# Fourteen gate tiles in seven pairs by seven products of quarters, in a fused two-block kernel

## The reference, cut to what matters

```python
proj = h @ w_in                      # 1024 -> 8456; the last 3072 columns are gm
ua = (ya * silu(ga)) @ w_up_a        # 512 -> 1024, likewise ub, uc
gates = sigmoid(gm.reshape(B, S, 3, D))
merged = gates[:, :, 0] * ua + gates[:, :, 1] * ub + gates[:, :, 2] * uc
x = x + merged @ w_o
# second block: mixers, x + y @ w_out, x + conv_ffn, then
x = x + sigmoid(x @ ple_w_gate) * (p @ ple_w_proj)
return rmsnorm(x) * final_norm_gain
```

## Time and profile before

| | us |
|---|---|
| median of 3 runs | 1244.85 (1244.41 to 1246.07) |
| time of the profiled execution | 1245.98 |
| its span, first to last instruction | 1244.2 |
| busy: PE, PEld, DVE, ACT, POOL | 1226.6, 980.8, 644.1, 553.3, 663.6 |

### The profile page before, as it was taken

The page is one execution under the profiler, slowest core; times in us unless marked ns, Lnnn a source line. Parts: engine busy times, 40 slices in busy tenths (PEclk is TensorE's granted clock), DMA queues, the critical chain, the costliest instruction groups (busy, mean ns, idle before and its releaser), DMA issues.

```text
span 1244.2 us, 17041 instructions
## 1 busy us (share of the span) xinstructions
PE 1226.6 (99%) x6262; PEld 980.8 (79%) x6262; DVE 644.1 (52%) x1101; ACT 553.3 (44%) x1078; POOL 663.6 (53%) x499
## 2 busy tenths in 40 slices
PE   9999999999999999999999999999999999999997
PEld 7977777777878888887787777878888888788886
DVE  5555326757624221144587655478999999100024
ACT  6355545676634333245634665533232323322344
POOL 6573222363256444445294556556776667655542
PEclk9999999999999999999999999999999999999999
DMA  7332222122233333353142123323333333433321
GB/s 247 92 91 71 62 66 61 51 71 75 60 85 94 101 93 95 87 166 112 41 116 62 42 75 93 102 68 102 96 90 95 94 102 89 119 95 98 96 81 68
DMA packets 62426, 112.14 MB, mean 90 GB/s; under 512 B 6856, under 2 KB 11464, under 8 KB 62344
## 3 DMA queue, kind: packets, MB, share of 16 engines
q1 hardware_dynamic: 62200, 111.06, 31.2%
q10 hardware_dynamic: 144, 0.00, 0.0%
HBM read 108.87 MB, written 2.16 MB: 89 GB/s over the span
## 4 chain that ended last, share of the span: by engine, by line
PE 91%; DVE 5%; ACT 3%; issue 1%; DMA 0%; POOL 0%; SPq 0%; DVEq 0%; ACTq 0%; POOLq 0%
PE pb L972 25%; PE pb L973 25%; PE pb L975 25%; PE pb L1131 2%; PE pb L1107 2%; PE pb L1074 1%; PE pb L1028 1%; PE pb L1026 1%; PE pb L1045 1%; PE pb L1047 1%; PE pb L1046 1%; PE pb L1096 1%; PE pb L996 1%; PE pb L992 1%; PE pb L994 1%
## 5 line engine op out<-in xcount | busy, mean ns | idle before, releaser
L2288 POOL TENSOR_TENSOR wlo<-raw,whi 128x512 fp32r<-128x512 f32 (+3 forms) x395 | 544.4, 1392 | 435.9 <-ACT whi L1313 435.6
L972 PE MATMUL pb<-HH,whi 128*128 128x512 f32 x968 | 389.7, 403 | 0.0
L973 PE MATMUL pb<-HL,whi 128*128 128x512 f32 x968 | 382.8, 395 | 0.0
L975 PE MATMUL pb<-HH,wlo 128*128 128x512 f32 x968 | 381.6, 394 | 0.0
L1313 ACT ACTIVATE whi<-raw 128x512 fp32r<-128x512 f32 (+3 forms) x395 | 234.7, 615 | 179.6 <-PE pb L975 138.6
L972 PEld LDWEIGHTS pb<-HH,whi 128*128 128x128 f32 x968 | 182.3, 188 | 47.2 <-issue 4.6
L973 PEld LDWEIGHTS pb<-HL,whi 128*128 128x128 f32 x968 | 182.1, 188 | 43.1 <-issue 2.9
L975 PEld LDWEIGHTS pb<-HH,wlo 128*128 128x128 f32 x968 | 182.0, 188 | 42.4
L1738 DVE SCALAR_TENSOR_TENSOR cv<-zf,vecs,cv 128x512 f32<-128x512 f32 x88 | 124.7, 1417 | 3.1
L1397 ACT ACTIVATE P<-P,stat 128x256 f32<-128x256 f32 (+3 forms) x96 | 50.6, 527 | 82.0 <-DVE stat L1862 59.6
L1729 DVE TENSOR_TENSOR X<-pb,X 128x512 f32<-128x512 f32 x24 | 16.6, 690 | 134.3 <-PE pb L975 133.9
(11 more groups left out here) (393 smaller groups left out, 1910.3 us busy)
## 6 DMA issues: line engine op xcount, KB each, us to landing
raw<-in_wall SPq DMA_DIRECT2D x368, 256.0 KB, 2.7
raw<-in_wall SPq DMA_DIRECT2D x8, 260.0 KB, 3.0
X<-in_xT SPq DMA_DIRECT2D x8, 256.0 KB, 5.4
X<-in_xT SPq DMA_DIRECT2D x2, 1024.0 KB, 7.6
outT<-PP SPq DMA_DIRECT2D x8, 256.0 KB, 2.5
raw<-in_wall SPq DMA_DIRECT2D x10, 192.0 KB, 2.4
raw<-in_wall SPq DMA_DIRECT2D x9, 128.0 KB, 2.2
cst<-in_cst SPq DMA_DIRECT2D x1, 832.0 KB, 7.4
```

The source lines that it names most:

```text
L972: pe.do.matmul(b, hi, xh[k], start=start, stop=False)
L973: pe.do.matmul(b, hi, xl[k], start=False, stop=False)
L975: m = pe.do.matmul(b, lo, xh[k], start=False, stop=stop)
L2288: g.do.tensor_tensor(lo, x, hi.bitcast(F32), ALU.subtract).then_inc(*up(name, point))
```

## The change

Fourteen of the fifteen gate tiles with d >= 3 are taken in seven pairs. For a pair the two weight tiles (1024 x 128 each) are cut along the inputs into halves: A11 and A12 of the one, A21 and A22 of the other; the activations into four quarters, inputs by tokens. Seven products of 512 inputs by 256 tokens give both tiles: the weight factors are A11, A22, S2, S1, S3, A12 and S4 (S1 = A21 + A22, S2 = S1 - A11, S3 = A11 - A21, S4 = A12 - S2). VectorE forms S1 to S4 in fp32 from the loaded quarters, ScalarE rounds them, GpSimd writes their low parts (VectorE that of S3). The sums of the activations are formed once, in four steps `t_sums`, by VectorE, ScalarE and GpSimd. The products go to banks 3 to 7; VectorE adds them in fp32 (`from_bank`), ScalarE takes the tanh. Blocks d = 4 and d = 6 hold two pairs in a row, d = 3, 5 and 7 one; gm(3, 0) stays a plain tile. The up tiles rotate through banks 0 to 2. SyncE refills a slot only after the sums that read it.

Other edits: kC runs its four high products, then the four with the low activations, then the four with low weights; the decay matmul has 64 rows, with zeros below the four; `sums` stands one step later; in the hgrn part the scaled copies (`query_copy`), the two halves of `inverse`, the levels, the first scores and the merges of scores move, and one of four near queries goes from VectorE to ScalarE; `square_a(2)` moves ahead of eight pauses; the gate of the last half tile is made by Exp, + 1, reciprocal and product on VectorE, and the tables are loaded once at the end, not three times.

```diff
+PAIRS = [((3, 1), (3, 2)), ((4, 0), (4, 1)), ((4, 2), (5, 0)), ((5, 1), (5, 2)), ((6, 0), (6, 1)), ((6, 2), (7, 0)),
+         ((7, 1), (7, 2))]
+PAIRS_OF = {3: (0,), 4: (1, 2), 5: (3,), 6: (4, 5), 7: (6,)}
+FACTORS = ("A11", "A22", "S2", "S1", "S3", "A12", "S4")
...
-        if d >= 3:
-            for j in range(3):
-                fm("win", GM + 1024 * j + P * d)
+        if d == 3:
+            fm("win", gm_col(3, 0))
+        for p in PAIRS_OF.get(d, ()):
+            for col, k0 in quarters(p).values():
+                fm4(col, k0)
...
+    def pair(self, p):
+        for i, x in enumerate("abcde"):
+            self.hold(3 + i, ("acc", p, x))
+        for x in FACTORS:
+            self.split_to(self.unit_of[p, x] + LOOK)
+            self.add("product7", p, x)
...
-            if i == 1:
+            if i == 2:
...
-            if d >= 3:
-                for j in range(3):
-                    gm(d, j)
+            if d == 3:
+                gm(3, 0)
+            for p in PAIRS_OF.get(d, ()):
+                self.pair(p)
...
-                take("main", ("up", n, d))
+                take("ups", ("up", n, d))
...
+            if d < 2:
+                add("t_sums", 2 + d)
...
+        copies = {(1, 4): ("query_copy", 0), (2, 1): ("inverse", 0), (2, 4): ("query_copy", 1), (2, 5): ("inverse", 1)}
         for t in range(3):
-            tile("bq", t)
+            tile("bq", t, lambda i: add(*copies[t, i]) if (t, i) in copies else None)
...
+            if k == 2:
+                add("query_copy", 2)
+                add("level", 4, 2)
+            if k == 5:
...
+            add("square_a", 2)
+            for _ in range(8):
...
+            def product7(p, x):
+                u = plan.unit_of[p, x]
+                hi, lo = whi[u % NS], wlo[u % NS]
+                acc = {"A11": "a", "A22": "e", "S2": "b", "S1": "c", "S3": "d", "A12": "a", "S4": "b"}[x]
+                b = ps("acc", p, acc)[:, 0:H]
+                if x == "A12":
+                    pe.wait_ge(*at("v0", p))
+                elif x == "S4":
+                    pe.wait_ge(*at("u2", p))
+                else:
+                    free(("acc", p, acc))
+                pe.wait_ge(*at("whi", u))
+                pe.wait_ge(*at("wlo", u))
+                for k in range(4):
+                    if x in T_AT:
+                        pe.wait_ge(*at("t_hi", k))
+                        pe.wait_ge(*at("t_lo", k))
+                        c = slice(H * T_AT[x], H * T_AT[x] + H)
+                        xh, xl = TH7[k][:, c], TL7[k][:, c]
+                    else:
+                        n, c = (k if x == "A11" else k + 4), (slice(H, T) if x == "S4" else slice(0, H))
+                        xh, xl = hh[n][:, c], hl[n][:, c]
+                    w = slice(P * k, P * k + P)
+                    begins = k == 0 and x != "A12"
+                    pe.do.matmul(b, hi[:, w], xh, start=begins, stop=False, skip_group_check=True)
+                    pe.do.matmul(b, hi[:, w], xl, start=False, stop=False, skip_group_check=True)
+                    m = pe.do.matmul(b, lo[:, w], xh, start=False, stop=k == 3, skip_group_check=True)
+                m.then_inc(*up("product", ("used", u), ("product7", p, x)))
...
+                def term(w, x, start, stop):
+                    for m in range(4):
+                        i = pe.do.matmul(ps("kC", m), w[u % NS][:, P * m:P * m + P], x[k], start=start, stop=stop)
+                        if stop and m < 3:
+                            i.then_inc(*up("proj", ("full", ("kC", m))))
+                    return i
+                if k == 0:
+                    for m in range(4):
                         free(("kC", m))
-                    pe.wait_ge(*at("whi", u))
-                    pe.wait_ge(*at("m_hi", k))
-                    pe.do.matmul(ps("kC", m), hi, mh[k], start=k == 0, stop=False)
-                    pe.wait_ge(*at("m_lo", k))
-                    pe.do.matmul(ps("kC", m), hi, ml[k], start=False, stop=False)
-                    pe.wait_ge(*at("wlo", u))
-                    i = pe.do.matmul(ps("kC", m), lo, mh[k], start=False, stop=k == KD - 1)
-                    if m == 3 or k == KD - 1:
-                        i.then_inc(*up("proj", ("full", ("kC", m)), ("used", u)))
+                pe.wait_ge(*at("whi", u))
+                pe.wait_ge(*at("m_hi", k))
+                term(whi, mh, k == 0, False)
+                pe.wait_ge(*at("m_lo", k))
+                term(whi, ml, False, False)
+                pe.wait_ge(*at("wlo", u))
+                term(wlo, mh, False, k == KD - 1).then_inc(*up("proj", ("used", u), *[("full", ("kC", 3))] * (k == KD - 1)))
...
-                        rows = slice(64 * s, 64 * s + 4)
+                        rows = slice(64 * s, 64 * s + 64)
...
+                load, factor = units[u]
+                if load is not None:
+                    n = int(plan.offset[load + 1] - plan.offset[load])
+                    x = raw[load % NR][:, 0:n]
+                    a.wait_ge(*at("raw", load))
+                else:
+                    n, x = T, S7[factor[1]]
+                    a.wait_ge(*at("s7", *factor))
                 if u >= NS:
                     a.wait_ge(*at("used", u - NS))
-                a.do.activation(whi[u % NS][:, 0:n], raw[u % NR][:, 0:n], ACT.Copy).then_inc(*up("whi", ("whi", u)))
+                a.do.activation(whi[u % NS][:, 0:n], x, ACT.Copy).then_inc(*up("whi", ("whi", u)))
...
+            def t_sums(kp):
+                a.wait_ge(*at("t_raw", kp))
+                a.do.activation(TH7[kp], TS7[kp], ACT.Copy).then_inc(*up("a_t7", ("t_hi", kp)))
+            def product7(p, x):
+                one, two = PAIRS[p]
+                g1, g2 = (GMs[(3 * d + j) % 9] for d, j in PAIRS[p])
+                b = ps("acc", p, "a")[:, 0:H]
+                if x == "A11":
+                    a.wait_ge(*at("product7", p, x))
+                    if p:
+                        a.wait_ge(*at("u3", p - 1))
+                    a.do.activation(U7, b, ACT.Copy).then_inc(*up("a_c7", ("v0", p)))
+                elif x == "A12":
+                    a.wait_ge(*at("product7", p, x))
+                    a.wait_ge(*at(*gm_free[one]))
+                    a.do.activation(g1[:, 0:H], b, ACT.Tanh, scale=0.5).then_inc(*up("a_gate", ("empty", ("acc", p, "a"))))
+                    a.wait_ge(*at("c21", p))
+                    a.do.activation(g2, g2, ACT.Tanh, scale=0.5).then_inc(*up("a_gate", ("gm", *two)))
+                elif x == "S4":
+                    a.wait_ge(*at("c12", p))
+                    a.do.activation(g1[:, H:T], g1[:, H:T], ACT.Tanh, scale=0.5).then_inc(*up("a_gate", ("gm", *one)))
...
+                if (d, half) == (7, 1):
+                    a.do.activation(y, ps("pg", d, half)[:, 0:H], ACT.Exp, scale=-1.0).then_inc(
+                        *up("a_gate", ("pg_exp",), ("empty", ("pg", d, half))))
+                    return
...
+                if half == 0:
+                    tables(LNEXP)
...
-                if half == 0:
-                    tables(EXPTANH)
...
+                v.do.memset(AK[:, :].bitcast(F32), 0.0).then_inc(*up("v_set", ("decay_zeros",)))
...
+            def split(u):
+                if units[u][1] is None:
+                    return
+                p, x = units[u][1]
+                arrived = {y: raw[plan.load_of[p, y] % NR][:, 0:T] for y in ("A11", "A12", "A21", "A22")}
+                def weights(name, one, two, op):
+                    v.do.tensor_tensor(S7[name], one, two, op).then_inc(*up("v_s7", ("s7", p, name)))
+                if x == "S2":
+                    for y in ("A22", "A21"):
+                        v.wait_ge(*at("raw", plan.load_of[p, y]))
+                    if p:
+                        v.wait_ge(*at("wlo", plan.unit_of[p - 1, "S4"]))
+                    weights("S1", arrived["A21"], arrived["A22"], ALU.add)
+                    v.wait_ge(*at("raw", plan.load_of[p, "A11"]))
+                    if p:
+                        v.wait_ge(*at("wlo", plan.unit_of[p - 1, "S2"]))
+                    v.wait_ge(*at("s7", p, "S1"))
+                    weights("S2", S7["S1"], arrived["A11"], ALU.subtract)
+                elif x == "S3":
+                    if p:
+                        v.wait_ge(*at("wlo", plan.unit_of[p - 1, "S3"]))
+                    weights("S3", arrived["A11"], arrived["A21"], ALU.subtract)
+                elif x == "A12":
+                    w = plan.unit_of[p, "S3"]
+                    v.wait_ge(*at("whi", w))
+                    v.do.tensor_tensor(wlo[w % NS][:, 0:T], S7["S3"], whi[w % NS][:, 0:T].bitcast(F32),
+                                       ALU.subtract).then_inc(*up("v_lo", ("wlo", w)))
+                elif x == "S4":
+                    v.wait_ge(*at("raw", plan.load_of[p, "A12"]))
+                    v.wait_ge(*at("wlo", plan.unit_of[p, "S1"]))
+                    weights("S4", arrived["A12"], S7["S2"], ALU.subtract)
+            def t_sums(kp):
```

(74 more changed lines are left out.)

165 lines of the change are left out of this document (103 added, 62 removed).

## The result

The kernel after takes 1250.78 us (1249.91 to 1252.69) against 1244.86 for the kernel before on the same chip: 1.0047 of it, 95% interval 1.0034 to 1.006. It is slower by 5.9 us, where 1235.8 was predicted. The profiled execution takes 1250.71 us with a span of 1248.9, 4.7 us more than before on both counts.

A forecast was written before the change was run, and what follows sets the result against it. TensorE, busy 99% of the span, was taken as the bound. Terms -9.6 + 0.85 + 5.2 + 0.5 + 0.3 - 4.3 - 2.9 - 1.6 + 2.5 = -9.05 from 1244.85 gave 1235.8 us; own range 1231 to 1240, wider 1228 to 1243.

The forecast's parts named there:

- The four t_sums: Activation sums, in up blocks d=0 and 1 and elsewhere: next lowered unit covered by 2.4 us; +0.3 us (0 to 4).
- Bank of the first pair: First product of pair 0 waits for the tanh that empties gm(3,0)'s bank 3: +0.85 us (0.8 to 1.5).
- Two pairs in a row: At d=4 and d=6 the second pair's first product waits for its bank, 2.6 us each: +5.2 us (0 to 6.6).
- Seven products: Each gate pair takes 84 matmuls of 256 columns, 9.79 us for 11.16; seven pairs: -9.6 us.
- Single pairs: At d=3, 5 and 7 the factors are covered by 0.7 us; +0.5 us for one that slips (0 to 7).
- Decay rows: Decay matmuls with 64 rows for 4 avoid row-count changes: 8 double groups x 0.54, -4.3 us.
- hgrn: Weight copies go ahead and first scores move later, removing waits on BV weights and qd: -2.9 us (0 to -2.9).
- sums and square_a: sums one step later, square_a(2) six steps earlier, removing waits for vC and G: -1.6 us (0 to -1.6).
- kC: New order puts eight products ahead of the first needing GpSimd's lowering; nothing taken, jointly with GpSimd's fills (-0.5 to +1.5).
- Tail: Last half tile's gate by Exp, +1, reciprocal, product; a reciprocal of 256 columns takes 2.6 us: +2.5 us (0.3 to 2.8).
- Rival B: Pairs bound by VectorE and GpSimd, 12.7 us each in place of 9.79: slower, 1250.5 us; chance 0.12.

The follow-up runs named there:

- run 6: The kernel after without the four t_sums; products that take a sum of activations read a plain quarter instead: 1237.44 us, 0.9946 of before.
- run 7: The kernel after with no pairs, all gate tiles plain, but the four t_sums kept though nothing reads them: 1242.82 us.
- run 12: The kernel after with one pair in each d from 4 to 7, tile 0 in bank 6, t_sums(2) and (3) inside d=3, old tail: 1232.55 us.
- run 8: The kernel after with 44 matmuls of 512 columns, results unread, put ahead of the first product's wait: 1248.85 us.
- run 11: The kernel after with one pair in each d from 3 to 7, tile 0 in bank 6, two t_sums moved, old tail: 1236.6 us.
- run 1: The kernel after without the pairs, the t_sums and the ring of three banks, all other edits kept: 1238.71 us, 0.9944 of before.
- run 13: Run 12's kernel with two pairs in d=4 and d=6, the second pair's accumulator a in banks 0 to 2, S4 in its own buffer: 1232.2 us.
- run 14: Run 13's kernel with S4 lowered by VectorE in place of GpSimd: 1231.39 us, 0.9886 of before.
- run 2: The kernel after with gm(3,0) in bank 6 in place of bank 3: 1245.82 us.

## Why the prediction was wrong

The gain of the products and the chain at the second pairs came as priced. The cover that it gave the sums did not hold, with it fell the term of the first bank, and a third term was missing.

- *The four t_sums, +0.3, "covered by 2.4".* This is the step that failed. The runs put 13.3 us on them (run 6). Two more sums in the up blocks d = 0 and 1 leave VectorE 10 us late and put GpSimd's lowerings behind two of 2.4 us. I counted the way to the next raw block, one round at a time, at the plain 0.69; the merges behind it took 2.9, and the lateness of d = 0 was carried into d = 1 and 2, whose 8.4 us of TensorE have no room for it: from the sum at 396.56 to that at 407.13 VectorE's round takes 10.6. Without pairs they cost 4.1 (run 7). Of the 13.3, 1.4 went in kB and d = 1, ahead of the first pair. That their place decides, and not the sums as such, is shown by runs 7 and 12: with no pair in d = 3 the stage of gm(3,0) takes 29.19 us with two of them in d = 0 and 1, and 25.12 with the same two inside it.
- *Bank of the first pair, +0.85.* The tanh was taken to start as its tile ends, as in the earlier trace rows. With what stood ahead of it in ScalarE's queue the stage lost 12.7; without the sums the wait is 0.7 (run 6).
- *Two pairs in a row, +5.2.* Waits of 2.35 and 3.05 for 2.6 each, by the chain as written. The clock behind the second adds 1.5 to 1.8: 7.5 over 2 x 28.1.
- *A wait's second price* was no term at all: TensorE at the lower clock behind it, about 2 us at the first pair (run 8), 1.5 to 1.8 at d = 6.
- *Seven products, -9.6.* 1.2 to 1.4 us per pair that runs free (runs 11 and 12) for 1.37. *Single pairs, +0.5:* 18.33 and 18.12 for 18.17.
- *Decay rows, -4.3:* -3.7 in the stages of branch c. *hgrn, -2.9:* -3.9 in the stage from BV on; both waits are gone, and where the last microsecond comes from was not traced. *sums and square_a, -1.6:* -1.2. *kC, 0:* -1.2. That run 1 came within 0.1 us of the sum of these is luck: the misses offset each other.
- *Tail, +2.5:* it came at 2.5, in part by luck. The reciprocal was 1.75 and not 2.6, and the +1 ahead of it took 0.84, not 0.42, so the last half came 2.1 us later on TensorE; 0.5 more came behind its wait of 4.4 us, where the last matmuls run at a granted clock of 0.50.
Rival B had nearly the measured time, 1250.5, by another way: it wanted 12.7 us in every pair. The single pairs at 9.7 to 10.0 us and run 11 refute that; only at d = 6, with the banks mended, does GpSimd's rate take part in setting the pace (runs 13 and 14). That the time came out near B's is luck. What is left open: why the clock fell behind waits of 2.2 us (run 2) and 3.05, and not behind 2.35 at d = 4.

## What to carry to other kernels

Work put on an engine that is idle half of the time on average still has to be placed where it is idle: read the engine's busy time in the very stretch, with contention, and carry its lateness from stage to stage before calling it covered. An operation that frees a bank has to be looked up in its engine's queue: what stands ahead of it, and whom that waits for. And a wait of TensorE can cost more than its length, by the clock behind it.
